# Idle products at the changes of stage: one full-height product, or a pair of half-height ones

## What is computed

```python
def first_block(x, p, norm_g, ...):
    for i in range(DEPTH):                      # 2 layers
        g = norm_g[i]
        x = x + FFN_RESIDUAL * rmsnorm(swiglu(rmsnorm(x, g[0]), ffn_w_in[i, 0], ffn_w_out[i, 0]), g[1])
        h = rmsnorm(x, g[2])
        j = i // N_MIXERS
        if i % N_MIXERS == 0:
            m = diff_attention(h, attn_w_qkv[j], attn_w_o[j], ...)
        else:
            m = s5_glu(h, lam_re, ..., ssm_w_glu[j], ssm_b_glu[j])
        x = x + rmsnorm(m, g[3])
        x = x + FFN_RESIDUAL * rmsnorm(swiglu(rmsnorm(x, g[4]), ffn_w_in[i, 1], ffn_w_out[i, 1]), g[5])
        gate = jax.nn.sigmoid(rmsnorm(x, g[6]) @ ple_w_gate[i])
        x = x + rmsnorm(gate * (p[i] @ ple_w_proj[i]), g[7])
    return x
```

## Time and profile before

| | |
|---|---|
| time, median of 3 runs | 1663.65 us (1663.43 to 1663.92) |
| the profiled execution: span | 1660.0 us |
| PE busy | 1630.5 us, 98% of the span, 8990 matmuls |
| PEld busy | 1370.2 us, 83% |
| DVE busy | 1100.5 us, 66% |
| ACT busy | 927.3 us, 56% |
| mean granted TensorE clock | 0.999 |

### The profile page before, as it was taken

The page is one execution under the profiler, slowest core; times in us unless marked ns, Lnnn a source line. Parts: engine busy times, 40 slices in busy tenths (PEclk is TensorE's granted clock), DMA queues, the critical chain, the costliest instruction groups (busy, mean ns, idle before and its releaser), DMA issues.

```text
span 1660.0 us, 22537 instructions
## 1 busy us (share of the span) xinstructions
PE 1630.5 (98%) x8990; PEld 1370.2 (83%) x8990; DVE 1100.5 (66%) x1567; ACT 927.3 (56%) x1559; POOL 165.8 (10%) x240
## 2 busy tenths in 40 slices
PE   9999999999999999999999999999999999999997
PEld 7888799788888877888878888788889889788886
DVE  5555667788877654969765556755567776655555
ACT  6555556655567585462465456645555444655555
POOL 0000001128301111900000000000000000000000
PEclk9999999999999999999999999999999999999999
DMA  6755443555555544441555555565544433555552
GB/s 239 259 199 197 171 165 127 185 196 184 195 187 189 212 169 152 177 179 52 199 179 190 187 183 188 190 223 196 180 175 178 144 112 127 184 203 178 197 184 102
DMA packets 50297, 295.93 MB, mean 178 GB/s; under 512 B 6072, under 2 KB 12688, under 8 KB 16528
## 3 DMA queue, kind: packets, MB, share of 16 engines
q1 hardware_dynamic: 49744, 293.86, 50.2%
q0 software_dynamic: 160, 0.52, 0.1%
q10 hardware_dynamic: 288, 0.11, 0.0%
HBM read 293.39 MB, written 1.09 MB: 177 GB/s over the span
## 4 chain that ended last, share of the span: by engine, by line
PE 88%; DVE 5%; ACT 4%; issue 1%; POOL 0%; DMA 0%; POOLq 0%; DVEq 0%; ACTq 0%
PE PS L2143 84%; PE PS L2365 2%; DVE wlo L1331 1%; PE PS L2288 1%; ACT SC L964 1%; ACT whi L747 1%; PE PS L2146 1%; PE PS L2580 0%; ACT wk L787 0%; DMA raw<-in_w 0%; DVE SC L1919 0%; DVE SC L1618 0%; DVE st L1602 0%; ACT wk L814 0%; DVE SC L1599 0%
## 5 line engine op out<-in xcount | busy, mean ns | idle before, releaser
L1337 DVE SCALAR_TENSOR_TENSOR wlo<-raw,ct,whi 128x512 fp32r<-128x512 f32 (+1 forms) x552 | 424.7, 814 | 258.4 <-ACT whi L751 258.3
L2143 PE MATMUL PS<-whi,xhi 128*128 128x512 f32 (+1 forms) x1312 | 505.6, 395 | 5.6 <-DVE wlo L1337 2.3
L751 ACT ACTIVATE whi<-raw,ct 128x512 fp32r<-128x512 f32 (+1 forms) x552 | 377.4, 734 | 225.8 <-PE PS L2143 169.1
L2143 PE MATMUL PS<-wlo,xhi 128*128 128x512 f32 (+1 forms) x1312 | 495.5, 387 | 0.0
L1331 DVE TENSOR_TENSOR wlo<-raw,whi 128x1024 fp32r<-128x1024 f32 x240 | 296.6, 1243 | 217.1 <-ACT whi L747 216.5
L2143 PE MATMUL PS<-whi,xlo 128*128 128x512 f32 (+1 forms) x1312 | 405.5, 387 | 0.0
L747 ACT ACTIVATE whi<-raw 128x1024 fp32r<-128x1024 f32 x240 | 251.7, 1057 | 259.1 <-PE PS L2143 192.7
L2143 PEld LDWEIGHTS PS<-whi,xhi 128*128 128x128 f32 x1312 | 246.0, 188 | 60.0 <-DVE wlo L1331 4.2
L2143 PEld LDWEIGHTS PS<-whi,xlo 128*128 128x128 f32 x1312 | 246.4, 188 | 51.3
L2143 PEld LDWEIGHTS PS<-wlo,xhi 128*128 128x128 f32 x1312 | 246.7, 188 | 47.5
L2143 PE MATMUL PS<-whi,hhi 128*128 128x512 f32 x544 | 173.3, 392 | 0.1
(11 more groups left out here) (282 smaller groups left out, 1503.5 us busy)
## 6 DMA issues: line engine op xcount, KB each, us to landing
raw<-in_w SPq DMA_DIRECT2D x263, 1024.0 KB, 4.8
gr<-in_rows SPq DMA_DIRECT2D x14, 512.0 KB, 3.8
SC<-scratch SPq DMA_DIRECT2D x5, 512.0 KB, 5.8
X<-in_x SPq DMA_DIRECT2D x2, 512.0 KB, 5.2
raw<-in_w SPq DMA_DIRECT2D x2, 512.0 KB, 6.9
SC<-scratch SPq DMA_DIRECT2D x4, 256.0 KB, 5.2
xn<-in_sc SPq DMA_DIRECT2D x2, 512.0 KB, 6.4
SC<-scratch SPq DMA_DIRECT2D x1, 1024.0 KB, 7.5
```

The lines of the kernel that those rows point to most:

```text
L751: e = a.activation(hi[:, f], src[:, f], ACT.Copy, scale=ct[:, c:c + 1])
L1337: e = v.scalar_tensor_tensor(lo[:, f], src[:, f], ct[:, c:c + 1], hi[:, f].bitcast(f32), MUL, SUB)
L2143: return pe.matmul(o, l, r, start=start, stop=stop)
```

## The change

Each idle product becomes two, one on rows 0 to 63 and one on rows 64 to 127 of the array, with the same 128 stationary columns and 512 moving columns; the first writes bank `b`, the second bank `b + 1`. The moving operand is taken from the second half of the unit (columns 512 to 1023) instead of the first. Counts, waits and places stay: every call of `fill_in` for `n` products issues `n` pairs. The line number of everything behind it grows by one.

```diff
                 hi, _ = weight(u)
                 for _ in range(n):
-                    mm(PS[:, b, :], hi[:, 0:128], hi[:, 0:512], True, True)
+                    for i, r in enumerate((slice(0, 64), slice(64, 128))):
+                        mm(PS[:, b + i, :], hi[r, 0:128], hi[r, 512:1024], True, True)
```

## The result

| | before | after |
|---|---|---|
| time, median of 15 runs each | 1663.67 us (1662.15 to 1666.22) | 1667.92 us (1665.42 to 1671.18) |
| ratio to before | | 1.0025, 95% interval 1.0018 to 1.0032 |
| profiled execution: span (time of that run) | 1660.0 us | 1667.3 us (1669.06 us) |
| PE busy, matmuls | 1630.5 us, 8990 | 1635.2 us, 9072 |
| ACT busy | 927.3 us | 926.6 us |

The account below looks back on a forecast made before the run. PE was taken to bound the kernel (88% of the chain that ended last). Pairs add 0 and switches 1.3 us: span 1660.0 becomes 1661.3, median 1663.65 + 1.3 = 1665.0 us, range 1663.6 to 1667.0.

Parts of the forecast that it names:

- What a pair takes: Two half-height products run side by side in one full-height product's time, 0.227 us: added 0, plus or minus 0.7 us overall.
- Rival 1: A pair's halves run one after the other, 18.6 us more streaming, giving 1681 us; chance 0.04.
- Entering and leaving: Each switch between 128-row and 64-row products costs about 0.20 us, paid twice by a stretch between two 128-row neighbours.
- Rival 2: A half's next weights wait for its product: 0.11 us exposed load per pair, 5.7 us, giving 1670.7; chance 0.04.
- Place by place: Switch costs summed over the eight idle stretches: 0.30 + 0.40 + 0.47 + 0.15 = 1.3 us.
- C: Six idle products around the SSM stage, ending just before a DVE result PE waits for; 0.05 us added.
- D and E: Stretches of 25 and 6 idle products around the SSM stage, on the chain; net 0.30 and 0.40 us added.
- H and I: Stretches of 8 and 4 idle products ahead of the mixers, on the chain; net 0.47 us added together.
- F and G: Stretches of 11 and 6 idle products ahead of the mixers, ending before a DVE wait; 0.05 us added each.
- A and B: Stretches of 12 and 4 idle products around the first attention, switches covered by waits for DVE; 0 added.
- rival 3: Half-height products count for less, so the clock drops to 1.2 GHz in the longest stretch: 1669 to 1673 us; chance 0.06.
- Nothing is moved, ... no DMA ... instruction changes: Whole kernel: no wait added, no DMA, DVE, ACT or POOL instruction changed; only 82 more matmuls and weight loads on PE.

Follow-up runs that it names:

- e_half: Changed kernel with only the first half (rows 0 to 63) of each pair, 82 half-height products instead of 164; 1666.56 us, ratio 1.0022 to the kernel before.
- y_rest2: Second measurement of the kernel with full-height products in the first two idle stretches, at the attention, and pairs in all others (66 pairs); 1664.61 us, ratio 1.0004.
- y_after64: Changed kernel plus eight tiny products behind the second warm-up, 64 PE instructions more than before ahead of the feed-forward part behind the attention; 1664.17 us, ratio 1.0004.
- x_ab: Pairs only in the first two idle stretches, at the attention (16 pairs), full-height products everywhere else as in the kernel before; 1666.04 us, ratio 1.0014.
- x_shift: Kernel before, with full-height idle products, plus eight tiny products behind the second warm-up (32 more PE instructions); 1665.79 us, ratio 1.0011.
- x_rest: Full-height products in the first two idle stretches, at the attention, pairs in all others (66 pairs); 1663.94 us, ratio 1.0002.
- e_after: The changed kernel run again with no edit; 1667.72 us, ratio 1.0026 to the kernel before.

## Why the prediction was wrong

It said 1665.0 us, in a range up to 1667.0, and the median came out at 1667.92. Point by point, by its own steps:

- **What a pair takes: held.** "Added 0" was taken between -0.013 and +0.013 us a pair. Pairs start 0.224 to 0.236 us apart in D, 0.229 in the mean, against 0.227 for one product: 0.002 added. Rival 1 (in series) is out by the start times and by `e_half`.
- **Entering and leaving: held.** 0.09 us of drain and 0.11 of exposed load were taken from two places of the trace of before; in the trace's own start times at D the first pair comes 0.319 us behind the last 128-row product, instead of 0.227, and the second pair 0.335 behind the first, where later ones are 0.224 to 0.236 apart; on the way out the first 128-row product comes 0.315 behind the last pair, and the second 0.533 behind the first, where later ones of that width are 0.429 apart. That is 0.09 and some 0.10 each way. Rival 2 (an exposed load in each pair) is out. The Trainium skill, "TensorE: Matmul & The Clock Gate", Part 3, has a weight load overlap products in flight only when the row group differs; the trace disagrees, since each half's next weights are loaded under its own product at 0.229 us a pair.
- **Place by place: held.** C 0.05 forecast, 0.04 found; D and E 0.70 forecast, 0.74 found; H and I 0.47 and 0.45; F and G 0.05 each, under 0.04 found; A and B nothing, nothing found until 380 us. Together 1.3, and `y_rest2`, without A and B, has a span longer by just that.
- **The clock: rival 3 is out where it was put.** In D the granted clock is 1.00. The short falls elsewhere are no more frequent with pairs than without (18 of 78 runs, 22 of 100).
- **"Nothing is moved, ... no DMA ... instruction changes": this is the step that failed.** It is true of the instructions that the program issues, and the argument took it for all that the DMA engines carry. They also carry the program, 71 blocks of 16 KB for PE. Each added matmul comes with a weight load, so A and B's 16 additional matmuls bring every later block forward by 32 instructions. One of them came to lie, 5 us earlier, on a 1 MB weight load for which ACT was already waiting, and two more on such loads behind it; in after each of the three took 1.1 to 1.4 us longer to land than in before, and in the four profiles that have them that was 3.9 to 4.4 us. So the price of A and B, put at 0, was the term that was wrong. How much it came to was chance: where the fetches fall beside those loads, as in `y_after64`, the same pairs cost 0.64 us, and the time lies inside the range. The instruction queue stood on the page of before; the prediction read only the queues of data. It could have been asked where the fetches fall, and whether ACT waits for a load there ([3.04 <-DMA raw<-in_w] in before).
- **The frame: mis-sized.** The 3.65 us by which the median stood above the profiled span were put down to "what lies around it". A run's time is only about 1.8 us above its own span; the profiled run of before was one of its faster ones, by some 1.9 us. The sum of the prediction was a difference, so this moved nothing in it; but a profile's difference, 7.2 us here, must not be read for that of the medians, 4.25.

**What stays open** is the exact share in the medians. By the ratios the stall alone is 2.3 us (`x_ab`, interval 0.8 to 3.8) or 1.8 (`x_shift`), less than the 3.9 to 4.4 in every profile that has it; the switches alone are 0.3 and 0.7 (`x_rest`, `y_rest2`; 1.3 lies within both intervals). Counting only runs with a mean clock of 0.998 or more, which leaves the falls out, after is 4.2 us above before (plus or minus 0.8), `x_ab` 2.8 (0.7), `x_rest` 0.5 and `y_rest2` 0.9 (0.7 each): 3.3 to 3.7 of 4.2 are then found in the two parts, and the rest lies within the intervals. That runs of before have such stalls at other loads, and that its two profiles happen to have none, would explain the smaller share, and is only argued. Open too is whether the second and the third fetch fall on their loads by the count alone, or also because the first has made those loads late: no run has one without the others.

## What to carry to other kernels

An instruction added to PE's stream was not only that instruction here: it moved the later fetches of PE's program, and these, by the times of the packets, share the DMA engines with the loads. Where a stage lives on loads that land just in time, look where the instruction queue's packets fall, and test a suspected shift with a few harmless instructions at the program's start, in two sizes. And an edit that costs nothing where it stands can still cost something 170 us further on, so price the place where the engine has no slack, not only the place of the edit.

## What the runs showed of the hardware

- Two products on the two halves of the rows, into two banks, run side by side in fp32r with their starts 0.003 to 0.004 us apart (D; at most 0.010 anywhere), and a pair takes 0.229 us in the mean for 512 columns (0.224 to 0.236), where one 128-row product takes 0.227.
- A change from 128-row products to 64-row ones costs 0.09 us at the first product and another 0.10 at the second, whose weight load is not hidden; the change back costs the same again.
- One 16 KB fetch of PE's program takes 0.89 to 0.95 us where it falls on the first of the three loads. Each of the three takes 5.97 to 6.28 us from issue to landing with a fetch on it (after, `e_after`, `x_shift`, `x_ab`) and 4.73 to 4.95 in the ten other traces; 15 of the 16 packets that close a load come together, and the last 0.4 to 1.4 us behind them. In after, PE then waits 3.2 us in all at four places, which leaves it 4.4 us later.
- Idle products on 64 rows alone were followed by a fall of the granted clock to 0.50 in F and G (mean clock 0.995 to 0.997 in 10 of 12 runs); pairs were not, any more than full-height products.
- Without E, 3 of 12 runs lost more than 10 us, at a mean clock of 0.99; in the profiled one of them PE had stood still for 0.90 us among small products, and 2.5 us later the clock went to half for 27.3 us.
